# In-projection and the border to attention: weight splits next to the convolutions, a reciprocal in two halves, and another order of the first operands of attention

## The reference

```
h    = rms_norm(x, g_pre) * (1 + scale) + shift          # scale, shift, gate: silu(c) @ w_mod + b_mod
q_c, kv_c, k_rope, z, xbc, dt_f, dt_b = split(h @ w_in)
ckv  = rms_norm(kv_c, g_kv);  q = rms_norm(q_c, g_q) @ w_uq
attn = attention(q, ckv @ w_ukv, rope(k_rope))           # 4 heads, one softmax over context and latent keys
xbc  = silu(depthwise_conv3(xbc));  ssm = two-way chunked scan of xbc, gated by silu(z), normed
out  = concat(attn, ssm) @ w_out;  then the norm, the gate and a SwiGLU FFN
```

## Time and profile before

| | us |
|---|---|
| three runs | 1747.73, 1750.08, 1751.28 (median 1750.08) |
| the profiled execution | 1751.78 |
| its span on the core | 1749.9 |
| PE busy | 1671.9 |
| DVE busy | 1039.5 |
| ACT busy | 725.8 |
| POOL busy | 76.9 |

### The profile page before, as it was taken

How to read it: one execution, slowest core, us unless ns; L and a number is a source line. 1 busy time by engine, 2 the same in 40 slices (tenths; PEclk the granted TensorE clock), 3 DMA queues, 4 the chain that set the end, 5 groups by cost and what they waited for, 6 DMA issues and landing times. The chain is left out here.

```text
span 1749.9 us, 24772 instructions
## 1 busy us (share of the span) xinstructions
PE 1671.9 (96%) x9795; PEld 1497.1 (86%) x9795; DVE 1039.5 (59%) x1581; ACT 725.8 (41%) x1208; POOL 76.9 (4%) x116
## 2 busy tenths in 40 slices
PE   6999899999889999999997999999999999999998
PEld 6787788878768888887887999999999999888886
DVE  5855656337755555574468555555555456466788
ACT  5652232324445344464555333333333333434453
POOL 0110000003300000000010000000000000000011
PEclk9999999999989999999999999999999999999999
DMA  9133242001310000023321122222222224773355
GB/s 372 73 133 125 105 149 94 26 33 48 108 33 19 1 13 1 21 83 138 126 104 49 70 92 88 94 87 80 99 101 93 79 88 145 258 237 95 121 164 187
DMA packets 76290, 176.33 MB, mean 101 GB/s; under 512 B 10352, under 2 KB 26944, under 8 KB 74128
## 3 DMA queue, kind: packets, MB, share of 16 engines
q1 hardware_dynamic: 72080, 169.75, 28.0%
q0 software_dynamic: 4096, 5.01, 0.9%
HBM read 131.02 MB, written 43.70 MB: 100 GB/s over the span
## 5 line engine op out<-in xcount | busy, mean ns | idle before, releaser
L409 PE MATMUL psF<-gv,gu_ring 128*128 128x320 f32 x1232 | 382.4, 310 | 9.2 <-issue 4.6
L410 PE MATMUL psF<-gv,gu_ring 128*128 128x320 f32 x1232 | 381.9, 310 | 0.0
L411 PE MATMUL psF<-gv,gu_ring 128*128 128x320 f32 x1232 | 381.8, 310 | 0.0
L409 PEld LDWEIGHTS psF<-gv,gu_ring 128*128 128x128 f32 x1232 | 232.3, 189 | 10.2 <-issue 9.2
L410 PEld LDWEIGHTS psF<-gv,gu_ring 128*128 128x128 f32 x1232 | 232.4, 189 | 0.0
L411 PEld LDWEIGHTS psF<-gv,gu_ring 128*128 128x128 f32 x1232 | 232.3, 189 | 0.0
L409 PE MATMUL psF<-d_w_ring,d_hid_ring 128*128 128x512 f32 x360 | 140.2, 389 | 0.0
L410 PE MATMUL psF<-d_w_ring,d_hid_ring 128*128 128x512 f32 x360 | 140.1, 389 | 0.0
L411 PE MATMUL psF<-d_w_ring,d_hid_ring 128*128 128x512 f32 x360 | 140.1, 389 | 0.0
L409 PE MATMUL psP<-hT_hi,win_hi 128*128 128x512 f32 (+1 forms) x336 | 123.0, 366 | 2.3 <-DVE hT_lo L184 1.6
L2424 ACT ACTIVATE hraw<-psF 128x320 f32<-128x320 f32 x130 | 56.8, 438 | 152.3 <-PE psF L411 150.8
(11 more groups left out here) (429 smaller groups left out, 3650.7 us busy)
## 6 DMA issues: line engine op xcount, KB each, us to landing
hid_variants<-hraw SPq DMA_DIRECT2D x77, 320.0 KB, 2.2
d_hid<-hid_variants SPq DMA_DIRECT2D x58, 320.0 KB, 3.0
m_wring<-in_w_mod SPq DMA_DIRECT2D x16, 1024.0 KB, 5.4
d_b<-in_w_down SPq DMA_DIRECT2D x44, 256.0 KB, 4.8
win_raw<-in_w_in SPq DMA_DIRECT2D x18, 512.0 KB, 5.6
w_mod_staged<-in_w_mod SPq DMA_DIRECT2D x16, 512.0 KB, 11.7
d_hid_more<-hid_variants SPq DMA_DIRECT2D x19, 320.0 KB, 3.0
raw_gu<-in_w_gate SPq DMA_DIRECT2D x11, 512.0 KB, 3.9
```

The source lines that it names most:

```text
L409: pe.matmul(out, w_hi, x_hi, start=first, stop=False, skip_group_check=onto)
L410: pe.matmul(out, w_hi, x_lo, start=False, stop=False, skip_group_check=onto)
L411: return pe.matmul(out, w_lo, x_hi, start=False, stop=last, skip_group_check=onto)
```

## The change

Three things change. (1) In the front, `invert` takes a range of columns. The first reciprocal runs over the first half in sumkv, and over the second half in tile q 1, behind that tile's splits; `normalise` for the keys' input follows the first copies of that tile. In tile q 2 the waits and turns of block 0 stand behind the second step k. (2) The high and low parts of a midway modulation step are made one tile earlier: on ACT before the wait for that tile's convolution, on DVE after the convolution, its row and its column, and before the normalisation of q, which moves behind them. `at_start` names a midway step that no earlier xbc tile has taken; there is none. (3) The last mix store and the stores of the states are issued by SP at the start of the attention phase, the mix store first. `landed` contains the weights of head 0 as well, in another order; the first block of q is split by row of 128; PE waits for each of these in its first block. The splits of later heads count accordingly.

```diff
@@ -467,6 +467,7 @@
         L.rows = in_hi
+        L.last_mixed, L.st_out = in_hi[:, 4:8, (NT - 1) * P:NT * P], st_in
         L.table = at("rope_table", "hT_lo", 6 * T * 4, [P, T])
@@ -554,6 +555,15 @@
...
+        def ahead(m):
+            return midway(m + 1 + (SEQUENCE[m + 1][0] == "sumq")) if m + 1 < len(SEQUENCE) else ()
+        def at_start(m):
+            before = [i for i in range(m) if SEQUENCE[i][0] == "xbc" and ahead(i) == midway(m)]
+            return () if before else midway(m)
@@ -647,13 +657,9 @@
...
                     sp.dma_start(in_hi[:, 3, 2 * N_CACHE:3 * N_CACHE], L.kr_s[:, T:NKEY]).then_inc(L.cache_in, 16)
-                if c == NT - 1:
-                    sp.wait_ge(fin_cp, 2)
-                    for d in range(2):
-                        sp.dma_start(L.outs["ssm"][0, 0, d].rearrange("(a h) p n -> (h p) a n", a=4),
-                                     st_in[:, d, :, :]).then_inc(fin_out, 16)
-                sp.wait_ge(mix_ready, c + 1)
-                sp.dma_start(quads(L.mixS[c]), zt(c)).then_inc(mix_stored, 16)
+                if c < NT - 1:
+                    sp.wait_ge(mix_ready, c + 1)
+                    sp.dma_start(quads(L.mixS[c]), zt(c)).then_inc(mix_stored, 16)
@@ -786,7 +792,7 @@
...
                     split(ct)
-                for n in midway(m):
+                for n in at_start(m):
                     mod.act_hi(act, MOD_EARLY + n)
@@ -800,6 +806,8 @@
...
                 if kind == "xbc":
+                    for n in ahead(m):
+                        mod.act_hi(act, MOD_EARLY + n)
                     n = xbc_order.index(i)
@@ -953,10 +961,10 @@
...
-            def invert(m):
+            def invert(m, cols=slice(0, T)):
                 dve.wait_ge(act_read, reads(m, False))
-                chain.link(dve.reciprocal(L.xbcT[:, 2, :], L.xbcT[:, 2, :]))
+                chain.link(dve.reciprocal(L.xbcT[:, 2, cols], L.xbcT[:, 2, cols]))
@@ -1050,8 +1058,9 @@
...
                     split(n)
+                for n in at_start(m):
+                    mod.dve_lo(dve, MOD_EARLY + n)
                 for n in midway(m):
-                    mod.dve_lo(dve, MOD_EARLY + n)
                     mod.dve_col(dve, MOD_EARLY + columns(m)[0])
@@ -1076,11 +1085,14 @@
...
                         take_u(n)
-                    invert(m)
-                    normalise(KKV, 6, C_GKV, kvn_ready)
+                    invert(m, slice(0, T // 2))
                 elif kind == "q" and i >= 1:
+                    if i == 1:
+                        invert(m - 1, slice(T // 2, T))
                     for n in itertools.chain(*U_AT[kind, i][2 - i:]):
                         take_u(n)
+                    if i == 1:
+                        normalise(KKV, 6, C_GKV, kvn_ready)
                 elif kind == "sumq":
@@ -1110,12 +1122,15 @@
...
                     dve.sem_inc(dve_read, 1)
-                    if SEQUENCE[m - 1][0] == "sumq":
-                        normalise(KQ, 3, C_GQ, qn_ready)
                 for n in after(m):
...
                     mod.dve_col(dve, MOD_EARLY + n)
+                if kind == "xbc":
+                    for n in ahead(m):
+                        mod.dve_lo(dve, MOD_EARLY + n)
+                    if SEQUENCE[m - 1][0] == "sumq":
+                        normalise(KQ, 3, C_GQ, qn_ready)
                 if kind == "kv" and i == 1:
@@ -1315,12 +1330,13 @@
...
                     for b, (c0, w) in enumerate(BLOCKS):
-                        if (kind, i) in U_AT and b == 0:
-                            pe.wait_ge(mod.col_ready, ct - 2)
-                            pe.wait_ge(mod.row_ready, ct - 1)
-                        for n in U_AT.get((kind, i), ((), (), ()))[b]:
-                            turn_u(n)
                         for k in range(KD):
+                            if k == (2 if (kind, i, b) == ("q", 2, 0) else 0):
+                                if (kind, i) in U_AT and b == 0:
+                                    pe.wait_ge(mod.col_ready, ct - 2)
+                                    pe.wait_ge(mod.row_ready, ct - 1)
+                                for n in U_AT.get((kind, i), ((), (), ()))[b]:
+                                    turn_u(n)
                             if (b, k) == (1, 4):
@@ -1567,12 +1583,18 @@
...
         part = lambda raw, hi, lo, c, w, sem, n: (raw, hi[:, :, c:c + w], lo[:, :, c:c + w], sem, n)
-        landed = ([part(rows[:, 4:7, c:c + w], L.qn_hi, L.qn_lo, c, w, L.q_in[b], w // 8) for b, (c, w) in enumerate(BLOCKS)] +
-                  [part(rows[:, 0:2, c:c + w], L.ckv_hi, L.ckv_lo, c, w, L.kv_in[b], w // 8)
-                   for b, (c, w) in enumerate(BLOCKS)] +
-                  [part(cache, L.ckv_hi, L.ckv_lo, T, N_CACHE, L.cache_in, 32),
+        q0, q1, q2 = (part(rows[:, 4:7, c:c + w], L.qn_hi, L.qn_lo, c, w, L.q_in[b], w // 8)
+                      for b, (c, w) in enumerate(BLOCKS))
+        kv0, kv1, kv2 = (part(rows[:, 0:2, c:c + w], L.ckv_hi, L.ckv_lo, c, w, L.kv_in[b], w // 8)
+                         for b, (c, w) in enumerate(BLOCKS))
+        first_w = [(raw[:], hi[:], lo[:], L.w_early, 64)
+                   for raw, hi, lo in ((wq_raw, wq_hi, wq_lo), (wk_raw, wk_hi, wk_lo), (wv_raw, wv_hi, wv_lo))]
+        landed = ([first_w[0]] + [tuple(x[:, k, :] for x in q0[:3]) + q0[3:] for k in range(KQ)] +
+                  [q1, first_w[1], kv0, q2, kv1, kv2, part(cache, L.ckv_hi, L.ckv_lo, T, N_CACHE, L.cache_in, 32),
                    (rows[:, 2, :], L.kr_hi[:, 0:T], L.kr_lo[:, 0:T], L.kr_in, 16 * NT),
-                   (rows[:, 3, 2 * N_CACHE:3 * N_CACHE], L.kr_hi[:, T:NKEY], L.kr_lo[:, T:NKEY], L.cache_in, 32)])
+                   (rows[:, 3, 2 * N_CACHE:3 * N_CACHE], L.kr_hi[:, T:NKEY], L.kr_lo[:, T:NKEY], L.cache_in, 32),
+                   first_w[2]])
+        N_ROPE, ROPE_AT, K_AT = 8, (1, 5, 8), (8, 9, 11)
         rc_ready, rb_ready, in_hi, in_lo = (L.sem("at_" + n) for n in ("rc", "rb", "in_hi", "in_lo"))
@@ -1636,11 +1658,18 @@
...
         def _(sp):
+            sp.dma_start(L.mixS[NT - 1].rearrange("p (a n) -> p a n", n=P), L.last_mixed).then_inc(L.mix_stored, 16)
+            for d in range(2):
+                sp.dma_start(L.outs["ssm"][0, 0, d].rearrange("(a h) p n -> (h p) a n", a=4),
+                             L.st_out[:, d, :, :]).then_inc(L.fin_out, 16)
             sp.wait_ge(L.mix_stored, 16 * NT)
...
             for h in range(1, HEADS):
-                sp.wait_ge(w_split, h)
+                if h == 1:
+                    sp.wait_ge(in_lo, len(landed))
+                else:
+                    sp.wait_ge(w_split, h - 1)
                 sp.dma_start(wq_raw[:], L.dram["w_uq"][h]).then_inc(wl, 16)
@@ -1657,16 +1686,12 @@
...
             def split(h):
-                if h == 0:
-                    act.wait_ge(L.w_early, 64)
-                else:
-                    act.wait_ge(wl, 32 * h)
-                    act.wait_ge(proj, n_proj(h))
+                act.wait_ge(wl, 32 * h)
+                act.wait_ge(proj, n_proj(h))
                 act.activation(wq_hi[:], wq_raw[:], ACT.Copy).then_inc(w_hi_r, 1)
...
                 if h % 2 == 0:
-                    if h >= 2:
-                        act.wait_ge(wvl, 16 * (h // 2))
+                    act.wait_ge(wvl, 16 * (h // 2))
                     act.activation(wv_hi[:], wv_raw[:], ACT.Copy).then_inc(w_hi_r, 1)
@@ -1701,7 +1726,6 @@
...
-            split(0)
             for src, hi, _, sem, n in landed:
@@ -1765,11 +1789,11 @@
             def split(h):
-                dve.wait_ge(w_hi_r, 2 * h + 2 + (h + 1) // 2)
+                dve.wait_ge(w_hi_r, 2 * h - 1 + (h + 1) // 2)
                 c.mark(dve.tensor_tensor(wq_lo[:], wq_raw[:], wq_hi[:].bitcast(F32), ALU.subtract))
...
                 if h % 2 == 0:
-                    dve.wait_ge(w_hi_r, 2 * h + 3 + h // 2)
+                    dve.wait_ge(w_hi_r, 2 * h + h // 2)
                     c.mark(dve.tensor_tensor(wv_lo[:], wv_raw[:], wv_hi[:].bitcast(F32), ALU.subtract))
@@ -1827,10 +1851,9 @@
...
-            split(0)
-            split_in(0, 3)
+            split_in(0, N_ROPE)
             rotate(0)
-            split_in(3, len(landed))
+            split_in(N_ROPE, len(landed))
             for kind in order[1:]:
@@ -1890,14 +1913,16 @@
...
                         continue
-                    if i == 0:
-                        pe.wait_ge(w_split, h + 1)
+                    if i == 0 and h >= 1:
+                        pe.wait_ge(w_split, h)
                     if i >= 5:
...
                     if h == 0 and kind in ("qrope", "k"):
-                        pe.wait_ge(in_lo, b + 1 if kind == "qrope" else (4, 5, 7)[b])
+                        pe.wait_ge(in_lo, (ROPE_AT if kind == "qrope" else K_AT)[b])
+                    elif h == 0 and kind == "v":
+                        pe.wait_ge(in_lo, len(landed))
                     c0, w = stage[kind][b]
@@ -1914,6 +1939,8 @@
...
                         for k in range(kn):
```

(2 more changed lines are left out.)

## The result

The changed kernel takes 1730.67 us (median of 4 runs, 1728.88 to 1733.6). The kernel before took 1749.69 us beside it (4 runs). The ratio is 0.9893 with a 95% interval of 0.9875 to 0.9912: 19.0 us less, where 16.5 were forecast. The profiled execution took 1731.76 us, its span is 1730.0.

A forecast was written before the change was run, and what follows sets the result against it. TensorE, busy 96% of the span, was taken to bound the kernel, so its idle and half-clock time counted. 4.3 + 4.2 + 2.3 + 5.75 = 16.5 us off 1750.08 gave a median of 1733.6, range 1729.5 to 1739.

The forecast's parts named there:

- Part 1: In-projection tiles q1 and q2: halving the first reciprocal around the splits saves 4.3 us, range 2.6 to 4.7.
- the clock's price: Tile q1, turn and product 3: without the 1.98 us gap the clock stays up, saving 1.7 us, bounds 0 and 1.7.
- The new wait at q2's second block: Tile q2, second block's turn: DVE's chain to copy 4 ends late, 0.4 us of new waiting, bounds 0 and 0.99.
- Part 2: Modulation weights made ahead: 4.2 us in tile xbc0 (bounds 2.6 and 4.2), 2.3 in later tiles (bounds 0 and 2.3).
- Part 3: Border to attention: ACT starts 1.65 us earlier and, with the new operand order, q projections start 5.75 us earlier.
- The last landing is not the limit: Border: the third q block is there by 485.6, before DVE wants its high part at 486.6.
- Half a border (1): Border to attention: only PE's earlier start is gained, 2.9 us instead of 5.75, time 1736.5; chance 12%.
- The clock that falls anyway (2): In-projection: the clock falls despite the removed gaps, so 1.7 + 1.5 us stay, time 1736.8; chance 6%.
- Gains given back downstream (3): Attention stage or the FFN's transfers give 8 us back, time 1741.6; chance 5%.
- Stutter at half clock (4): Border: PE's pieces stutter and the clock stays at 1.2 GHz until the first scores, time 1758.5; chance 3%.
- No change (5): Whole kernel: gains meet waits that were not seen, time 1750; chance 3%.
- Stretches with gaps of 1.21 us or less show none: In-projection: argument against the clock falling anyway, that gaps of 1.21 us or less show no clock drop.

The follow-up runs named there:

- e1_halves: The kernel before with only the first reciprocal in halves around the splits and q2's turn two steps later; 1744.63 us, ratio 0.9968.
- e2_ahead: The kernel before with only the midway modulation weights' high and low parts made a tile earlier; 1742.12 us, ratio 0.9958.
- e5_turn_k0: The changed kernel with q2's first waits and turns back at the head of block 0; 1730.61 us, ratio 0.9894.
- e6_norm_first: The changed kernel with DVE's normalisation of q back ahead of the low part of the modulation weights; 1734.54 us, ratio 0.9917.
- e3_border: The kernel before with only the last stores moved to the attention phase and its first operands reordered; 1743.38 us, ratio 0.996.
- e9_again: The changed kernel once more, unedited, to see what repeats between executions; 1730.84 us, ratio 0.989.
- e4_order: The kernel before with only the new order of attention's first operands, the stores left where they were; 1747.36 us, ratio 0.998.
- e11_whole_after: The changed kernel with the first reciprocal whole, behind tile q1's splits and ahead of its copies; 1733.68 us, ratio 0.991.

## Why the prediction was right

**Part 1** (4.3 us forecast): A gave 4.39 after and in e1_halves. The 1.98 us of waiting went, and PEclk is 1.00 in 139 to 143. But the clock's price, which entered the sum in full (1.7 us, with bounds of 0 and 1.7), was luck in part: e2_ahead kept the wait and lost nothing to the clock, and turn and product 3 took 2.68 us there (142.11 to 144.79) against 4.17 before. The term holds for executions such as the one it was read from. Further, the halves cost 4.15 us each against 4.1 by proportion. The new wait at q2's second block, charged with 0.4, is a gap of some 0.3 around the turn at 148.52. The 0.99 us moved behind two steps were worth 0.78 (e5_turn_k0), within 0.2 of what the sum had for it (0.99 less 0.4).

**Part 2** (4.2 + 2.3 = 6.5 us): B gave 6.98 after, 6.94 in e2_ahead. The 2.63 us went with the fall of the clock behind them, and L361's waits fell to the 1.2 us that the forecast left. That the gain in xbc0 needs DVE's new order, and not only ACT's, is shown by e6_norm_first.

**Part 3** (5.75 us): E gave 5.88 after and 5.34 in e3_border, with two steps off in opposite directions. ACT's start moved by 1.96 us (2.35 to 0.39) and not by 1.65: the forecast had kept the 0.67 us between SP's end and ACT's start, and they became 0.4. Why they did, no run shows. "The last landing is not the limit" was false in the profiled run: ACT idled 2.04 us for the third q block, and PE 0.43 us behind it. The forecast had its issue 4.0 us behind the last copy and 2.7 us for its landing; it was issued after 3.0 and took 4.4. The block came 7.46 us after ACT's last copy, as in e3_border (7.58), but after 5.65 to 7.11 in the seven later kernels. PE's first piece came 0.3 us early, by the 3.61 us of idleness against 3.9, and the full clock came back 3.9 us behind it, where the forecast had 4.6. Over the kernels with both the order and the moved stores that was 3.5 to 5.9 us, and so E's 5.88 is one draw.

**The sum** was 16.5, the three parts gave 17.25, and e1 to e3 together 17.4 in their medians. The median fell by 19.0, and the span of the profiled runs by 19.9.

The measured 1730.67 us lie in the stated range, 1729.5 to 1739, but the working does not earn that lower end. With every bound at its fast end the sum is 4.7 + 4.2 + 2.3 + 5.75 = 16.95 us, which gives 1733.1. The measured time is 2.5 us below this, and lay inside by room that no term accounts for.

What the forecast lacked is the clock in places that no part was meant to change. At the first out-projection PE idles 1.35 us in the kernel before and in e3_border alike. The windows show what followed, in the kernel before and then in e3_border:

```profile
801.00:805.00 4.00, 3.02 (x7) 2.48 (x8) 2.53 (x3) 2.73 (x5) 0.10 (x1) 0.60 0.50 154
```

```profile
796.00:801.00 5.00, 3.92 (x17) 3.28 (x18) 3.11 (x4) 3.32 (x5) 0.10 (x1) 1.00 0.58 175
```

The same holds at the start of the scan, where equal windows, from 6 us ahead of the scan's first exponents to 8 us behind them, give 0.63 before and 0.88 after:

```profile
386.00:400.00 14.00, 10.67 (x31) 6.77 (x31) 7.34 (x11) 3.59 (x4) 2.69 (x3) 0.63 0.24 92
```

```profile
374.00:388.00 14.00, 9.95 (x36) 5.99 (x36) 7.91 (x12) 3.59 (x5) 2.69 (x3) 0.88 0.23 86
```

Such places differ from one execution to the next: D is 84.17 in e9_again and 84.67 after, one and the same kernel, and goes from 84.17 to 85.58 over the kernels of the table, though none edits it. They may not be chance alone. At the start of the scan the low clock lasts 10.2 us in all five kernels that lack a part (before and e1 to e4) and 3.4 to 6.8 us in the eight that have all three. The two waits of PE ahead of it are the same in both groups (1.12 and 1.13 us), and the cause stays open. Nor is it sure that the whole is worth more than its parts. It is 1.6 us better in the medians, but by the ratios the parts give 19.9 us and the whole 18.7, and the intervals hold both.

**The rivals.** Half a border (1) would have E near 21.4; it is 18.42. The clock that falls anyway (2) would show PEclk under 1 at 139 to 143 and 205 to 209; it is 1.00. Its premise, that the fall need not come from the gap alone, is borne out all the same for q1 by e2_ahead. Gains given back downstream (3): the three stretches behind E are 0.21, 0.71 and 0.25 us shorter than before. Stutter at half clock (4): the clock was back by 473, 4 us after PE's start at 468.96. No change (5) is excluded by the interval.

The forecast's reason on the clock was weaker than its sum. "Stretches with gaps of 1.21 us or less show none" is true of the 1.21 us at 201.02 and false of the trace. At the start of the scan the clock of the kernel before fell at 388.8, 0.3 us behind this wait of 1.13 us, the second of its kind in a row:

```profile
388.49 1.73 PE L1384 MATMUL psP<-xw,chunks_lo 128*128 128x256 f32 x4 [1.13 <-DVE xw L1138]
```

Nor does the length decide above that. A fall went with 1.35 us in the kernel before and not in e3_border, it followed 1.98 us in both of these and not in e2_ahead, and none followed 1.58 (e6_norm_first) or 1.84 us (e11_whole_after). Only the 2.63 us of tile xbc0 had a fall behind them in all four kernels that have them (before, e1_halves, e3_border, e4_order; 2.65 us in e3_border). The Trainium skill ("TensorE: Matmul & The Clock Gate", section "Why this matters for your kernels") warns only of idle gaps above some 3 us; the trace of before shows a fall behind 1.98 and 2.63 us, so the measurement decides against it. No run here shows what decides in the single case.

## What to carry to other kernels

A short operation that feeds the bottleneck engine is worth moving ahead of a long one on the same queue, and a long one is worth cutting in half if the short ones then fit between: both gains could be read off one timeline of the helping engine and came out within 0.5 us of the forecast, though 1.5 us of part 1's was clock that an execution without the edit can keep too. Count a gap on TensorE at its own length plus what the granted clock shows behind it, but call the second part a chance and not a sum. A stretch that ends behind a restart of TensorE carries the accident of when the clock returns; compare two versions at the first piece of work as well. At a border between blocks, ask which engine issues last and what the first consumer needs first.

## What the runs showed of the hardware

- A reciprocal of 1280 columns takes 8.15 us and one of 640 columns 4.15, some 6.4 ns a column. Two halves take 0.15 us more than the whole, so cutting it is nearly free.
- With the stores out of SP's queue ahead of the border, ACT started 0.39 us after its last copy in after and e3_border and 0.73 in e9_again, against 2.35 before. In the kernel before, SP's issues of the two state stores (0.98 us) and the mix store (0.64 us) stood between, and ACT started 0.67 us behind the second. In e9_again SP's last load ended after ACT's copy, and ACT started 0.4 us behind it.
- The half-clock time behind PE's restart at the border does not follow the length of the idleness: it lasted 3.9 us (after) and 5.9 us (e3_border) behind 3.61 us, 3.2 us behind 6.37 (e4_order), and 4.8 us behind 8.12 (before).
- One and the same wait, 1.98 us at the same place, was followed by a fall of the clock in before, e3_border and e4_order, and by none in e2_ahead. The stretch A was 1.5 to 2.6 us longer with the fall.
- The landing of one load differs between executions of one kernel: the third q block took 4.4 us from its issue in after and 2.8 us in e9_again, with the same stores ahead of it.
